# Twenty of the early rows' dots go from VectorE to TensorE in a decoder block; routings, row packing and the second norm change groups

## The reference, cut to what matters

```python
def peer_ffn(xn, wq, sub_keys, u_tab, v_tab):
    q = (xn @ wq).reshape(B, S, PEER_HEADS, 2, PEER_HALF)          # 256 tokens, 8 heads, 2 halves of 128
    s = jnp.einsum('bshpd,hpnd->bshpn', q, sub_keys)
    top_v, top_i = lax.top_k(s, 16)
    cand_v, cand_i = lax.top_k(top_v[..., 0, :, None] + top_v[..., 1, None, :], 16)   # of 16 x 16
    experts = i1 * 128 + i2
    gates = jax.nn.softmax(cand_v, axis=-1)
    act = jax.nn.gelu(einsum('td,tkd->tk', x, u_tab[experts]))     # 128 experts a token, rows of 2048
    return einsum('tk,tkd->td', gates * act, v_tab[experts])
```

## Time and profile before

| | us |
|---|---|
| median of 3 runs | 2686.42 (2684.03 to 2688.29) |
| the profiled execution | 2683.64 |
| its span | 2681.6 |
| VectorE busy in the span | 2062.4 (77%) |
| TensorE busy | 2163.6 (81%) |
| dots on early rows (L2218), 192 | 434.7, mean 2.275 |
| gathers (L836), 192 | 411.3, mean 2.142 |

### The profile page before, as it was taken

One profiled execution on the slowest core, in us unless ns is written; L12 is line 12 of the kernel. 1 busy time (PEld: TensorE's weight loads), 2 busy tenths in 40 slices (PEclk: granted clock), 3 DMA queues, 4 the chain that ended last, 5 costly groups with the idle time before them and its releaser, 6 DMA issues.

```text
span 2681.6 us, 33701 instructions
## 1 busy us (share of the span) xinstructions
PE 2163.6 (81%) x12145; PEld 1874.2 (70%) x12145; DVE 2062.4 (77%) x2612; ACT 1265.2 (47%) x2004; POOL 692.9 (26%) x343
## 2 busy tenths in 40 slices
PE   8999999999999899999999600003419999999997
PEld 7997789999988788889889500003317777777775
DVE  7885556566654855664468999999998999999999
ACT  4464544444444443454355301775835444444444
POOL 1000000000000100010001487886862343343341
PEclk9999999999999999999999855556759999999999
DMA  7453565555465455564457898999988999999997
GB/s 235 134 159 119 179 195 165 158 157 157 156 214 187 157 187 188 174 207 154 135 179 289 319 390 333 388 411 400 406 332 330 421 422 421 421 421 421 421 421 311
DMA packets 273965, 728.95 MB, mean 272 GB/s; under 512 B 21192, under 2 KB 164768, under 8 KB 215856
## 3 DMA queue, kind: packets, MB, share of 16 engines
q1 hardware_dynamic: 226432, 385.65, 41.3%
q0 software_dynamic: 46912, 340.81, 31.5%
q10 hardware_dynamic: 496, 0.84, 0.1%
HBM read 725.14 MB, written 2.10 MB: 271 GB/s over the span
## 4 chain that ended last, share of the span: by engine, by line
PE 57%; DVE 23%; DMA 16%; issue 2%; ACT 2%; POOL 0%; DVEq 0%; ACTq 0%; POOLq 0%
PE bank L419 19%; PE bank L441 18%; DVE b_u_ring L2218 14%; PE bank L468 10%; DMA b_v_raw<-in_peer_v 7%; DMA b_late_row<-in_peer_v,b_idx_all 4%; DMA b_late_row<-in_peer_u,b_idx_all 4%; PE bank L1729 3%; PE bank L1741 2%; PE bank L1517 1%; DVE b_hN L2292 1%; DVE b_late_row L2285 1%; PE bank L1401 1%; DVE b_v_lo L2268 1%; ACT b_v_hi L1289 1%
## 5 line engine op out<-in xcount | busy, mean ns | idle before, releaser
L405 DVE TENSOR_TENSOR b_w_both<-b_raw,b_w_both 128x1024 fp32r<-128x1024 f32 x464 | 566.4, 1239 | 443.5 <-ACT b_w_both L400 442.4
L400 ACT ACTIVATE b_w_both<-b_raw 128x1024 fp32r<-128x1024 f32 x464 | 484.0, 1057 | 551.0 <-PE bank L419 214.1
L836 POOL DMA_INDIRECT b_u_ring<-in_peer_u,b_idx_all x192 | 411.3, 2142 | 154.3 <-DVE b_dots L2218 81.2
L2218 DVE CUSTOM_DVE_ANT_0 b_u_ring<-b_u_ring,b_xnN 128x2048 f32<-128x2048 f32 x192 | 434.7, 2275 | 0.0
L1729 PE MATMUL bank<-b_v_hi,b_e_parts 128*128 128x512 f32 x1536 | 381.2, 397 | 33.7 <-DVE b_e_parts L2273 22.0
L1289 ACT ACTIVATE b_v_hi<-b_v_raw 128x1024 fp32r<-128x1024 f32 x256 | 257.1, 1052 | 299.7 <-DVE b_v_lo L2268 150.1
L1729 PEld LDWEIGHTS bank<-b_v_hi,b_e_parts 128*128 128x128 f32 x1536 | 282.9, 189 | 125.1 <-DVE b_e_parts L2273 34.8
L419 PE MATMUL bank<-b_w_both,b_act_both 128*128 128x512 f32 x1536 | 355.0, 391 | 2.5 <-ACT b_w_both L400 2.5
L419 PEld LDWEIGHTS bank<-b_w_both,b_act_both 128*128 128x128 f32 x1536 | 288.5, 189 | 62.7 <-ACT b_w_both L400 3.0
L441 PE MATMUL bank<-b_act_both,b_w_both 128*128 128x256 f32 x2688 | 328.4, 284 | 0.0
L441 PEld LDWEIGHTS bank<-b_act_both,b_w_both 128*128 128x128 f32 x2688 | 324.2, 192 | 1.6 <-issue 1.3
(11 more groups left out here) (315 smaller groups left out, 2418.3 us busy)
## 6 DMA issues: line engine op xcount, KB each, us to landing
b_v_raw<-in_peer_v SPq DMA_DIRECT2D x128, 1024.0 KB, 11.2
b_raw<-in_w_in SPq DMA_DIRECT2D x208, 512.0 KB, 4.4
b_raw<-in_w_proj_dsa SPq DMA_DIRECT2D x32, 512.0 KB, 4.4
b_raw<-in_w_proj_gla SPq DMA_DIRECT2D x32, 512.0 KB, 4.2
b_raw<-in_w_xk SPq DMA_DIRECT2D x32, 512.0 KB, 3.3
b_raw<-in_w_out SPq DMA_DIRECT2D x32, 512.0 KB, 3.3
b_raw<-in_w_xv SPq DMA_DIRECT2D x32, 512.0 KB, 4.6
b_raw<-in_w_xq SPq DMA_DIRECT2D x32, 512.0 KB, 3.3
```

The lines of the kernel that those rows point to most:

```text
L400: act.activation(w_hi[:, q], raw[:, UQ * c + q], ACT.Copy).then_inc(w_high, 1)
L405: dve.tensor_tensor(w_lo[:, q], raw[:, UQ * c + q], w_hi[:, q].bitcast(F32), ALU.subtract).then_inc(w_split, 1)
L836: pool.indirect_dma_start(u_ring[:, s], None, u_rows, bass.IndirectOffsetOnAxis(ap=idx_all[:, at:at + 1], axis=0)).then_inc(u_landed[s], 16)
L2218: dve.tensor_tensor_reduce(u, u, xnN[:, g // PEER_H], 1.0, 0.0, ALU.mult, ALU.add, dots[:, g * PTOP + k:g * PTOP + k + 1]).then_inc(sem("d ...
```

## The change

`TURNED_ROWS` lists twenty rows: k = 3, 7, 11, 15 of groups 1, 2 and 3, k = 7 and 15 of groups 4, 5 and 6, k = 3 and 11 of group 7. Their dots leave VectorE. Once, after the last scores, TensorE transposes `xnN[:, 0]` in four quarters (`turn_quad`) into banks 2 to 5, and ScalarE copies them to `xn_turned`. For each turned row TensorE waits for its landing, transposes it in four quarters through the same banks (16 transposes), ScalarE copies each quarter to one of two halves of `row_turned` (`copy_row`), and TensorE multiplies them (16 matmuls of 128x128, `dot_quad`) into bank 6 or 7. The diagonal of that product holds the dots. VectorE's `add_diagonal` multiplies the bank with the identity and sums, 128x128. It stands at the place of the next turned row, the last one behind row 127. POOL waits for a turned row's slot on `turned_in`, its fourth quarter's transposes, and counts `dotted` in the new order otherwise.

`ROUTES_IN` gives group 1 routings 3 and 4, group 2 routings 5 and 6 and group 3 routing 7. `norm_rows(1)` moves from before group 0's last rows to before group 2, `pack_rows` to the end of group 3, the seeds of banks 4 to 7 behind the last turned row. The tile `distances` moves to another address, and `xn_turned`, `row_turned` and `diagonal` are new.

```diff
@@ -71,6 +71,11 @@
 assert 2 * EARLY_PAIRS == P
 ROWS_HELD = 2
 MARKED_FROM, MARKED_A_GROUP = 4, 9
+TURNED_ROWS = tuple(g * PTOP + k for g, ks in ((1, (3, 7, 11, 15)), (2, (3, 7, 11, 15)), (3, (3, 7, 11, 15)), (4, (7, 15)),
+                                               (5, (7, 15)), (6, (7, 15)), (7, (3, 11))) for k in ks)
+QUADS = 4
+ROUTES_IN = ((2,), (3, 4), (5, 6), (7,))
+BLOCKS_TURNED, BLOCKS_COPIED, ROWS_TURNED = 24, 16, 8
 UNITS_BY_GROUP = {8: 12, 9: 16, 10: 4}
 COLS_BY_GROUP = {10: 8, 11: 8}
 
@@ -288,7 +293,10 @@
     folded = sb("folded", [D], RAW + 96 * K)
     squared = sb("squared", [D], SCR + 8 * K)
     row_hot = sb("row_hot", [ROWS_HELD, UNIT, NKEYS], MRG)
-    distances = sb("distances", [2, 2, UNIT, NKEYS], MRG + 8 * K)
+    distances = sb("distances", [2, 2, UNIT, NKEYS], RAW + 112 * K)
+    xn_turned = sb("xn_turned", [KT, P], MRG + 8 * K)
+    row_turned = sb("row_turned", [2, KT // QUADS, P], MRG)
+    diagonal = sb("diagonal", [P], MRG + 4 * K)
     col_hot = sb("col_hot", [ROWS_HELD, UNIT, NKEYS], RAW + 112 * K)
     oct_rows = sb("oct_rows", [ROWS_HELD, UNIT, NKEYS], MRG)
     oct_cols = [sb(f"oct_cols{o}", [UNIT, NKEYS], at + 2 * n * K) for o, (at, n) in enumerate(
@@ -644,6 +652,30 @@
         same = [m for m in range(n) if row_slot[m] == row_slot[n]]
         return same[-1] if same else None
 
+    dot_order = []
+    for n in range(EARLY * PTOP):
+        if n not in TURNED_ROWS:
+            dot_order.append(n)
+        elif n != TURNED_ROWS[0]:
+            dot_order.append(TURNED_ROWS[TURNED_ROWS.index(n) - 1])
+        if n == PEER_H * PTOP - 1:
+            dot_order.append(TURNED_ROWS[-1])
+
+    def dotted_at(n):
+
+        return dot_order.index(n) + 1
+
+    def quad(r, q):
+
+        return QUADS + QUADS * r + q
+
+    def row_used(eng, n):
+
+        if n in TURNED_ROWS:
+            eng.wait_ge(sem("turned_in"), BLOCKS_TURNED + quad(TURNED_ROWS.index(n), QUADS))
+        else:
+            eng.wait_ge(sem("dotted"), dotted_at(n))
+
     def places(count, first, grow):
 
         place, back = [], []
@@ -673,10 +705,7 @@
 
     def routes_in(g):
 
-        extra = GROUPS - EARLY - 2
-        if extra == 0 or g < 3:
-            return [r for r in (g + 2,) if r < GROUPS]
-        return list(range(g + 2, g + 3 + extra)) if g == 3 else [r for r in (g + 2 + extra,) if r < GROUPS]
+        return list(ROUTES_IN[g]) if g < len(ROUTES_IN) else [r for r in (g + GROUPS - EARLY,) if r < GROUPS]
 
     def weights_of(b):
 
@@ -831,7 +860,7 @@
                     pool.wait_ge(units_used, unit(END, 0))
                 before = row_before(at)
                 if before is not None:
-                    pool.wait_ge(sem("dotted"), before + 1)
+                    row_used(pool, before)
                 s = row_slot[at]
                 pool.indirect_dma_start(u_ring[:, s], None, u_rows,
                                         bass.IndirectOffsetOnAxis(ap=idx_all[:, at:at + 1], axis=0)
@@ -1229,6 +1258,14 @@
             act.activation(spread_shared[:, :, UNIT * o:UNIT * (o + 1)], bank[2 + o % 2].rearrange("p (i t) -> p i t", t=UNIT),
                            ACT.Copy).then_inc(sem("spread_copied"), 1)
 
+        def copy_row(r):
+
+            for q in range(QUADS):
+                act.wait_ge(sem("turned_in"), BLOCKS_TURNED + quad(r, q) + 1)
+                wait(act, sem("rows_turned"), ROWS_TURNED + quad(r, q) - 2 - QUADS + 1)
+                act.activation(row_turned[:, q % 2].rearrange("p k t -> p (k t)"), bank[2 + q], ACT.Copy
+                               ).then_inc(sem("copied_in"), 1)
+
         def mark_unit(u):
 
             wait(act, sem("marked"), u - 1)
@@ -1274,7 +1311,7 @@
 
         def expert_gelu(lo, hi):
 
-            act.wait_ge(sem("dotted"), hi)
+            act.wait_ge(sem("dotted"), max(dotted_at(n) for n in range(lo, hi)))
             return act.activation(w_all[:, lo:hi], dots[:, lo:hi], ACT.Gelu_apprx_tanh)
 
         def value_high(i):
@@ -1318,16 +1355,26 @@
         sims_out(6)
         peer_out(7)
         sims_out(7)
-        pack_rows()
+        for q in range(QUADS):
+            act.wait_ge(sem("turned_in"), BLOCKS_TURNED + q + 1)
+            act.activation(xn_turned[:, QUADS * q:QUADS * (q + 1)].rearrange("p k t -> p (k t)"), bank[2 + q], ACT.Copy
+                           ).then_inc(sem("copied_in"), 1)
         made = 0
         for g in range(8):
             if g == MARKED_FROM:
                 turn_over(0, (0, 2))
-            if g >= MARKED_FROM:
-                for u in range(made, min(made + MARKED_A_GROUP, HALF)):
+            rows = [r for r, n in enumerate(TURNED_ROWS) if n // PTOP == g]
+            marked = min(MARKED_A_GROUP, HALF - made) if g >= MARKED_FROM else 0
+            for i, r in enumerate(rows):
+                for u in range(made, made + marked * (i + 1) // len(rows) - marked * i // len(rows)):
                     mark_unit(u)
                     made = u + 1
-            for r in routes_in(g):
+                if i == len(rows) - 1 and len(routes_in(g)) > 1:
+                    gate_exp(routes_in(g)[0])
+                copy_row(r)
+            if g == MARKED_FROM - 1:
+                pack_rows()
+            for r in routes_in(g)[-1:]:
                 gate_exp(r)
         act.wait_ge(sem("marked"), HALF)
         expert_gelu(0, PEER_H * PTOP).then_inc(sem("gelu_ready"), 1)
@@ -1758,10 +1805,46 @@
                                    skip_group_check=True)
             mm.then_inc(sem("tile_used"), 1)
 
+        def turn_quad(i, src):
+
+            wait(pe, sem("copied_in"), BLOCKS_COPIED + max(0, i - QUADS + 1))
+            for b in range(KT // QUADS):
+                kt = i % QUADS * (KT // QUADS) + b
+                mm = pe.transpose(bank[2 + i % QUADS][:, b * P:(b + 1) * P], src[:, kt * P:(kt + 1) * P], ident)
+            mm.then_inc(sem("turned_in"), 1)
+
+        def dot_quad(r, q):
+
+            pe.wait_ge(sem("copied_in"), BLOCKS_COPIED + quad(r, q) + 1)
+            for b in range(KT // QUADS):
+                kt = q * (KT // QUADS) + b
+                mm = pe.matmul(bank[6 + r % 2][:, 0:P], row_turned[:, q % 2, b], xn_turned[:, kt], start=(kt == 0), stop=(kt == KT - 1))
+            mm.then_inc(sem("rows_turned"), 1)
+
+        def dot_turned_row(r):
+
+            n = TURNED_ROWS[r]
+            pe.wait_ge(*row_landed(n))
+            for q in range(QUADS):
+                turn_quad(quad(r, q), u_ring[:, row_slot[n]])
+            if r >= 2:
+                pe.wait_ge(sem("dotted"), dotted_at(TURNED_ROWS[r - 2]))
+            for q in range(QUADS):
+                dot_quad(r, q)
+
         pe.wait_ge(sem("sims_ready"), PEER_H)
-        seed(range(4, 8)).then_inc(sem("seeded"), 1)
+        pe.wait_ge(sem("dotted"), 1)
+        for q in range(QUADS):
+            turn_quad(q, xnN[:, 0])
+        before_tables = sum(n < MARKED_FROM * PTOP for n in TURNED_ROWS)
+        for r in range(before_tables):
+            dot_turned_row(r)
         pe.wait_ge(sem("routed"), PEER_H)
         turn_tables(0, (isel_all[:, 0], isel_all[:, 1]), 0, 0)
+        for r in range(before_tables, len(TURNED_ROWS)):
+            dot_turned_row(r)
+        pe.wait_ge(sem("dotted"), dotted_at(TURNED_ROWS[-1]))
+        seed(range(4, 8)).then_inc(sem("seeded"), 1)
         pe.wait_ge(sem("weights_ready"), 1)
         turn_tables(1, (w_all,), 0, 0)
         pe.wait_ge(sem("doubled"), 1)
@@ -2211,12 +2294,25 @@
             link(dve.tensor_tensor(gates, gates, parts, ALU.mult))
 
         def dot_row(g, k):
+            n = g * PTOP + k
+            if n in TURNED_ROWS:
+                if n != TURNED_ROWS[0]:
+                    add_diagonal(TURNED_ROWS.index(n) - 1)
+                return
             if g == PEER_H and k == 0:
                 dve.wait_ge(sem("rows_packed"), 3)
-            dve.wait_ge(*row_landed(g * PTOP + k))
+            dve.wait_ge(*row_landed(n))
             u = u_ring[:, row_slot[g * PTOP + k]]
             dve.tensor_tensor_reduce(u, u, xnN[:, g // PEER_H], 1.0, 0.0, ALU.mult, ALU.add, dots[:, g * PTOP + k:g * PTOP + k + 1]
                                      ).then_inc(sem("dotted"), 1)
+            if n == PEER_H * PTOP - 1:
+                add_diagonal(len(TURNED_ROWS) - 1)
+
+        def add_diagonal(r):
+
+            dve.wait_ge(sem("rows_turned"), ROWS_TURNED + QUADS * (r + 1))
+            dve.tensor_tensor_reduce(diagonal, bank[6 + r % 2][:, 0:P], ident, 1.0, 0.0, ALU.mult, ALU.add,
+                                     dots[:, TURNED_ROWS[r]:TURNED_ROWS[r] + 1]).then_inc(sem("dotted"), 1)
 
         def group(g, k=0):
 
@@ -2333,9 +2429,10 @@
             if n % 5:
                 dot_row(0, done)
                 done += 1
-        norm_rows(1)
         group(0, done)
         for g in range(1, EARLY):
+            if g == 2:
+                norm_rows(1)
             if g == PEER_H:
```

## The result

The changed kernel takes 2667.68 us in the median of four runs (2664.6 to 2670.22), the kernel before 2687.31 in the median of four (2684.03 to 2688.29; the prediction had three of them, 2686.42); the ratio is 0.9929, with a 95% interval of 0.9918 to 0.9941. Faster was right, and 2667.7 lies inside the range of 2648 to 2674, but 28 us were forecast and 19.6 came. The profiled run took 2664.6 with a span of 2662.9, so 18.7 us less span than before. It is this span that is taken apart here.

A forecast was written before the change was run, and what follows sets the result against it. VectorE was taken to bound the stretch; its work alone would save 36.9 us, but gathers come next and, with 1.5 and 2 us added, leave 28: 2686.4 - 28 = 2658.4 us, range 2648 to 2674.

The forecast's parts named there:

- VectorE bounds the kernel before: Before the change, VectorE's dots run without waits and set the stretch's end, 41.44 us a group.
- VectorE's work after: Groups 1 to 7: VectorE's own work falls from 305.1 to 268.2 us, 36.9 less if it alone decided.
- The rows are late next, at 2.49 us each: Groups 3 to 7: DMA gathers decide, 39.9 us a group, ending 5.3 us later than VectorE alone would.
- Rival A: VectorE stays the bound because rows come faster or the ring's lead is larger; 2651 us, chance 0.14.
- rival B: Gathers cannot go faster than now, 2.61 us a row at 401 GB/s; gain about 19, 2667 us, chance 0.12.
- So rows 48 to 52 are there or under way, and 75 rows have to come: At group 3's start, rows 53 to 127 remain to be gathered: 75 x 2.49 = 186.8 us, to 1797.6.
- The surcharge of 1.5 + 2 us for unevenness and first waits: Added to groups 3 to 7: 1.5 us for DMA and POOL unevenness, 2 for first handoff waits; end about 1803.6.
- ScalarE keeps up: Groups 4 to 6: ScalarE needs 41.3 us against 39.9, lagging 1.4 a group, yet reaches the GELU with about 3 to spare.
- rival D: Slower: copy_row holds ScalarE between marks in groups 4 to 7, eating the gain from about 7.7 us each; 2696 us, chance 0.05.
- rival C: TensorE stays at 1.2 GHz in groups 1 to 3, diagonals come late, some 15 us lost; 2673 us, chance 0.10.
- One gather for each dot: POOL issues one gather per VectorE dot, a fifteenth at k = 7, the sixteenth when VectorE stands still; 2.50 us a row.
- Groups 8 to 11: They keep 16 dots and one routing each, bound by VectorE at 41.44 us: nothing gained or lost.

The follow-up runs named there:

- the divided copies: Changed kernel, but in groups 4 to 7 ScalarE makes one marked unit between a turned row's second and third copy; 2660.2 us, ratio 0.9898.
- the second run: The same kernel with a marked unit between the second and third copy, run once more on another chip; 2662.44 us, ratio 0.9910.
- the short marks: Changed kernel, but marked units from the third on leave out their eight distance instructions (part of the computation missing); 2664.15 us, ratio 0.9918.

## Why the prediction was right, and where its size was off

- **VectorE bounds the kernel before**: right. Half the bytes moved nothing (0.9999).
- **VectorE's work after**: right in every term, within 0.4 us. Dots 172, diagonals 0.27 to 0.29 us each in VectorE's time (0.27 taken), norm_rows 2.27 bare (2.3), groups 1 and 2 together 84.6 us with 0.6 of waits (84.2), busy time 33.6 and 37.6 in groups 3 to 6 (33.7, 37.5).
- **The rows are late next, at 2.49 us each**: right. Groups 5 and 6 take 39.7, and with ScalarE out of the way groups 4 to 7 run at 421 to 422 GB/s. Rival A (no waits, 37.5 a group) and rival B (400 GB/s) are both out as to the mechanism, though B's time, 2667, is the measured one: its price was right by chance, since its 401 GB/s for every row isn't what happened: 421 to 422 where nothing stalled, 379 in the group of the stall.
- **"So rows 48 to 52 are there or under way, and 75 rows have to come"**: this is the step that failed. They were under way, which isn't there. The prediction read a landing time of 8.9 us in the earlier trace rows and then counted a gather as done when it was issued. TensorE's timeline dates row 51, the first turned one of group 3 (its transposes start when it lands), and the gathers of that moment took 10.1 us to land:

```profile
1614.93 2.75 PE L1813 MATMUL bank<-b_consts,b_u_ring 128*128 128x128 f32 x16 [3.04 <-DMA b_u_ring<-in_peer_u,b_idx_all]
```

From there 76 rows x 2.49 + 2.5 for the last dot and diagonal give 1806.6 for the end of group 7, against 1800.1 in the prediction's sum without its surcharges. Of these 6.5 us, 1.2 are group 3's later start (1612.03 for 1610.8, of which 0.8 is group 1's later start in this trace), and 5.3 the rows counted as present. The corrected count holds where ScalarE isn't late: with the divided copies row 51 landed at 1619.35, it says 1811.1, and group 8's first dot came at 1812.83; in the second run 1618.22, 1809.9 and 1811.26; with the short marks 1617.14, 1808.8 and 1811.03.
- **The surcharge of 1.5 + 2 us for unevenness and first waits**: 7.7 us were lost in the changed kernel (1806.6 to 1814.35), 1.3 to 2.2 in the three kernels just named. The difference is ScalarE.
- **ScalarE keeps up, "41.3 a group against 39.9: 1.4 us of lag a group", "about 3 us to spare"**: the size of a group was right (9 x 3.43 + 2 x 4.9 + 0.7 = 41.4), the copies' 4.8 too (4.9 to 5.1), and the conclusion wrong. The prediction asked whether ScalarE would be in time for gate_exp and for the GELU (it was: no step of VectorE waited for gate_exp, and ScalarE stood 2.92 us before the GELU), and forgot the nearest client: the diagonals themselves, and behind them the slot of the next turned row. ScalarE was late for these from 1653 on; the first wait of VectorE for it was 6.18 us, and GpSimd's 7.16. That is rival D's mechanism, at the copy time of 4.9 us from which the prediction had said that nothing would come of it; it decides not from 7.7 us (D's own terms give 8.8: (222.2 - 1.4 - 33.7 - 39) / 3 is 49.4 a group, less 31.7, halved), but as soon as a group's sum is above the rows' pace, after as many groups as the slack of one diagonal lasts.
- Together: 1.2 + 5.3 + (7.7 - 3.5) = 10.7 us late at the end of group 7, 1814.35 for 1803.6. Behind it 1.4 us came back, 0.1 in groups 8 to 11 and 1.3 in what follows, which is inside the spread of that part between traces and so luck (the seeds hid at the end of group 7, as forecast, and took 3.70 us there instead of 6.85). So 28 - 10.7 + 1.4 = 18.7.
- **TensorE** (rival C): out. The granted clock was 0.80 to 0.83 of 2.4 GHz in groups 1 to 3, and no diagonal waited there; a turned row kept TensorE busy for 7.3 to 7.4 us (29.25 and 29.53 for four), as the 7 to 8 taken. The rule of the Trainium skill that was weighed, in "TensorE: Matmul & The Clock Gate", section "Part 4: PE-mode transpose", that transposes don't count for the clock, can't be decided here: two thirds of the steps are matmuls.
- **One gather for each dot**: right, and worth more than the 1.5 us it was given. At 14 dots a group it stood only 0.5 us below the bytes' limit, and at 15 with one gap groups took 41.4 to 42.1. The fifteenth gather goes at k = 7, and the sixteenth only while VectorE stands still at the group's end, as the prediction had it: the 0.94 us gathers at 1729.4 and 1769.1 go inside waits of 1.86 and 1.93 us. That a diagonal, whose first input lies in PSUM, holds no gather up is borne out. Of the changed kernel's twenty, fifteen run during a long gather, which ends 0.81 us behind the dot before it like all others, and four during a short one, which stays at 0.94 us:

```profile
1562.64 0.28 DVE L2314 CUSTOM_DVE_ANT_0 b_diagonal<-bank,b_consts 128x128 f32<-128x128 f32 x1
...
1562.79 0.94 POOL L865 DMA_INDIRECT b_u_ring<-in_peer_u,b_idx_all  x1 [0.30 <-issue]
```

The Trainium skill, "SBUF — State Buffer", section "SBUF: two separate sides", has a VectorE operation with two SBUF inputs and a GpSimd operation that reads SBUF exclude each other, and the traces agree, with 1.9 to 3.0 us beside dots and 0.94 beside a diagonal. The same section's 432 GB/s for the DMA engines was not reached, 422 being the most over any group here.
- **Groups 8 to 11**: 42.30, 41.43, 41.44 and 41.5, where the kernel before has 42.42, 41.45, 41.45 and 41.5: nothing gained or lost, as said.
- **The signs named**: the 172 dots, the twenty short operations and 11.7 us of waits for rows in groups 3 to 7 (3 to 12) came as forecast. So did rival D's sign, a wait of VectorE for a diagonal and a ScalarE without idle time in groups 4 to 7. The last dot ended at 1981.2, not about 1970.

## What to carry to other kernels

When work is moved off the engine that bounds a stretch, count the next resource from the first item that has *landed*, not from what is issued; with a landing time of 10 us and 2.5 us an item, a full ring is four items short (both figures are of this kernel). For each helper engine that serves in program order, compare its sum for a period with the period of the new bound, not of the old one, and list everyone who waits for each of its results, the freeing of buffers above all: 1.5 us over in each group stayed invisible for three groups and then made a wait of 6.2 us and a group 4.5 us longer. A wait inside a helper's step (1.8 and 1.1 us for another engine) is best filled with a piece of its other work; that alone brought 5.3 and 5.9 us here.

## What the runs showed of the hardware that was not expected

- A DMA share of 1.00 doesn't mean that DMA is the bound. At 401 GB/s (kernel before) halving the bytes changed nothing, at 402 GB/s with sixteen turned rows GpSimd was the engine without slack; in groups 4 to 7 the bytes were the bound at 421 to 422 GB/s, by the 0.5 us a group that halving them gave. The GB/s tell what the share doesn't.
- Gathers of half the size went out no faster: a gather that GpSimd begins without a wait, beside a VectorE dot, takes 1.9 to 3.0 us whether its rows have 8 or 4 KB, and 0.94 us in a gap.
- The same stretch ahead of group 1 ended at 1526.4 to 1531.5 us in traces of kernels that don't differ there, and a run's median moved by 2 us between two chips (2660.2 and 2662.4). Differences of 2 us in this kernel are read from the stretch, not from the total.
